# Combining the expert sums at the end of a mixture-of-experts layer on VectorE and GpSimd

## The reference, cut to what matters

```python
def trunk_layer(x, cond, lw, rope_a, rope_b, ctx):
    ...
    sh1, sc1, g1, sh2, sc2, g2 = jnp.split(mod, N_MOD, axis=-1)
    ...
    x = x + g1 * a
    h = rmsnorm(x, lw['norm2_g']) * (1 + sc2) + sh2
    b, s, d = h.shape
    x = x + g2 * moe_ffn(h.reshape(b * s, d), lw).reshape(b, s, d)
    return x, ctx_out

def moe_ffn(h, lw):
    ...
    routed = routed_experts(h, idx, w, lw['w_e1'], lw['w_e3'], lw['w_e2'])
    return routed + swiglu(h, lw['w_s1'], lw['w_s3'], lw['w_s2'])
```

## Time and profile before

| | |
|---|---|
| median of 3 runs | 1682.61 us (1682.14 to 1683.42) |
| the profiled execution, its own time | 1688.23 us |
| its span, first to last instruction | 1686.5 us |
| TensorE busy | 1541.8 us (91%) |
| VectorE busy | 1015.5 us (60%) |
| ScalarE busy | 723.2 us (43%) |
| GpSimd busy | 669.1 us (40%) |
| granted TensorE clock, mean | 0.973 |

### The profile page before, as it was taken

How to read it: one execution, slowest core, us unless ns; L and a number is a source line. 1 busy time by engine, 2 the same in 40 slices (tenths; PEclk the granted TensorE clock), 3 DMA queues, 4 the chain that set the end, 5 groups by cost and what they waited for, 6 DMA issues and landing times.

```text
span 1686.5 us, 25448 instructions
## 1 busy us (share of the span) xinstructions
PE 1541.8 (91%) x7703; PEld 1170.6 (69%) x7704; DVE 1015.5 (60%) x1601; ACT 723.2 (43%) x1067; POOL 669.1 (40%) x728
## 2 busy tenths in 40 slices
PE   8799798889989999999988999999999999999991
PEld 2678687778879999984544676666666666666660
DVE  1966688666666546544753666666656655665554
ACT  2523344334333222211212666666666655655550
POOL 0444277232214223310253355544546545544440
PEclk9899899989999999999999999999999999999996
DMA  9311100000006546527146888999999999999975
GB/s 326 106 61 43 38 1 1 1 1 1 1 26 176 150 133 217 150 80 255 38 188 218 294 280 295 323 352 341 338 336 356 335 328 339 353 331 327 336 241 199
DMA packets 126834, 333.71 MB, mean 198 GB/s; under 512 B 21140, under 2 KB 76568, under 8 KB 102040
## 3 DMA queue, kind: packets, MB, share of 16 engines
q1 hardware_dynamic: 104536, 288.09, 46.4%
q0 software_dynamic: 21440, 42.04, 10.2%
q10 hardware_dynamic: 784, 2.65, 0.4%
HBM read 316.54 MB, written 47.95 MB: 216 GB/s over the span
## 4 chain that ended last, share of the span: by engine, by line
DMA 30%; PE 18%; DVE 2%; issue 2%; SPq 1%; another core or an unknown queue 1%; ACT 1%; ACTq 0%; DVEq 0%; POOL 0%; POOLq 0%
DMA mem<-in_w_e 29%; PE psum L1746 4%; PE psum L2227 4%; PE psum L1608 2%; PE psum L2208 2%; PE psum L2210 2%; PE psum L2209 2%; SPq L2134 1%; PE psum L2216 1%; PE psum L1966 1%; DMA sums<-mem,si 1%; PE psum L1767 0%; DVE e_wlo L2322 0%; DMA mem<-sums 0%
## 5 line engine op out<-in xcount | busy, mean ns | idle before, releaser
L2322 DVE TENSOR_TENSOR e_wlo<-mem,e_whi 128x2048 fp32r<-128x2048 f32 x140 | 314.6, 2289 | 174.9 <-ACT e_whi L1922 174.8
L1922 ACT ACTIVATE e_whi<-mem 128x2048 fp32r (+1 forms) x140 | 260.5, 1908 | 104.7 <-SPq L2127 79.3
L2227 PE MATMUL psum<-mem 128*128 x560 | 253.4, 595 | 10.8 <-ACT mem L2290 10.8
L2164 POOL TENSOR_TENSOR held<-nhalf 1x1 f32<-1x1 f32 x206 | 144.5, 702 | 295.0 <-ACT mem_h L2282 144.2
L2208 PE MATMUL psum<-e_whi,e_xhi 128*128 128x512 f32 x560 | 228.1, 407 | 2.9 <-DVE e_xlo L2330 2.9
L2210 PE MATMUL psum<-e_wlo,e_xhi 128*128 128x512 f32 x560 | 222.2, 397 | 0.0
L2209 PE MATMUL psum<-e_whi,e_xlo 128*128 128x512 f32 x560 | 222.0, 397 | 0.0
L2227 PEld LDWEIGHTS psum<-mem 128*128 128x128 f32 x560 | 100.9, 190 | 114.7 <-issue 114.5
L1494 POOL TENSOR_TENSOR w_lo<-mem,w_hi 128x1024 fp32r<-128x1024 f32 x30 | 77.5, 2603 | 159.1 <-ACT w_hi L1438 159.1
L2208 PEld LDWEIGHTS psum<-e_whi,e_xhi 128*128 128x128 f32 x560 | 105.7, 189 | 25.7 <-issue 2.4
L2210 PEld LDWEIGHTS psum<-e_wlo,e_xhi 128*128 128x128 f32 x560 | 105.5, 188 | 25.6
(11 more groups left out here) (326 smaller groups left out, 3296.6 us busy)
## 6 DMA issues: line engine op xcount, KB each, us to landing
mem<-in_w_e SPq DMA_DIRECT2D x192, 1024.0 KB
mem<-in_w_mod SPq DMA_DIRECT2D x24, 1024.0 KB, 12.1
mem<-in_w_in SPq DMA_DIRECT2D x16, 512.0 KB, 4.6
mem<-in_w_in SPq DMA_DIRECT2D x3, 2048.0 KB, 8.7
sums<-mem SPq DMA_DIRECT2D x10, 512.0 KB
mem<-sums SPq DMA_DIRECT2D x10, 512.0 KB, 8.1
mem<-in_x_sample SPq DMA_DIRECT2D x8, 512.0 KB, 11.1
mem<-in_w_oa SPq DMA_DIRECT2D x8, 512.0 KB, 5.9
```

The costliest lines, as they stand in the source:

```text
L1922: act.activation(wHi13[b][:, a].rearrange("p k n -> p (k n)"), raw, ACT.Copy).then_inc(se["h13"], 1)
L2164: pool.tensor_tensor(held[:, c:c + 1], nhalf[0:1, 0:1], nhalf[0:1, 0:1], ALU.add)
L2227: mm = pe.matmul(pY[:, c * 512:(c + 1) * 512], gT[:, f, :], rows_.rearrange("p o w -> p (o w)"), start=(f == 0), stop=(f == 1))
L2322: dve.tensor_tensor(wLo13[b][:, a].rearrange("p k n -> p (k n)"), raw, wHi13[b][:, a].rearrange("p k n -> p (k n)").bitcast(F32), ALU.subt ...
```

## The change

All five tiles of the first sum are now multiplied by the gate and added to the residual as they land, on VectorE. The second sum is multiplied by the gate and added in a second pass: its tiles 2, 3 and 4 by VectorE, its tiles 0 and 1 by GpSimd, behind its last scatter. GpSimd counts on a new semaphore `s_cp`. The stores are issued in the order 2, 0, 3, 1, 4, each waiting on the engine that finishes that tile. Tiles 2 to 4 take four operations instead of three: the gate is applied to each sum rather than to their sum.

```diff
--- before.py
+++ after.py
@@ -1914,7 +1914,9 @@
     s_yt = [[sem(f"s_yt{b}{t}") for t in range(NT)] for b in range(2)]
     s_cb = sem("s_cb")
     s_cc = sem("s_cc")
+    s_cp = sem("s_cp")
     s_fin = sem("s_fin")
+    TAIL_POOL, TAIL_DVE = (0, 1), (2, 3, 4)
 
     def round_w13(act, slot, b, a):
 
@@ -2198,6 +2200,12 @@
                 due(pool, guard(3), scatter)
 
             run(pool, step)
+            for n, t in enumerate(TAIL_POOL):
+                pool.wait_ge(s_yt[1][t], 16)
+                pool.tensor_tensor(yt[1][t], yt[1][t], g2b[:, min(t, 1), :], ALU.mult).then_inc(s_cp, 1)
+                pool.wait_ge(s_cp, 2 * n + 1)
+                pool.wait_ge(s_cb, 2 * t + 2)
+                pool.tensor_tensor(yt[0][t], yt[0][t], yt[1][t], ALU.add).then_inc(s_cp, 1)
 
         @block.tensor
         def _(pe):
@@ -2304,8 +2312,11 @@
 
 
             run(act, step)
-            for t in range(NT):
-                act.wait_ge(s_cc, t + 1)
+            for t in (2, 0, 3, 1, 4):
+                if t in TAIL_DVE:
+                    act.wait_ge(s_cc, TAIL_DVE.index(t) + 1)
+                else:
+                    act.wait_ge(s_cp, 2 * TAIL_POOL.index(t) + 2)
                 dst = O["yp"][0] if t == 0 else O["ys"][0, (t - 1) * P:t * P, :]
                 act.dma_start(dst, yt[0][t]).then_inc(s_fin, 16)
             act.wait_ge(s_fin, 16 * NT)
@@ -2347,24 +2358,16 @@
 
             lo_w13(0, 0, 0)
             run(dve, step)
-            for t in range(2):
+            for t in range(NT):
                 dve.wait_ge(s_yt[0][t], 16)
                 dve.tensor_tensor(yt[0][t], yt[0][t], g2b[:, min(t, 1), :], ALU.mult).then_inc(s_cb, 1)
                 dve.wait_ge(s_cb, 2 * t + 1)
                 dve.tensor_tensor(yt[0][t], yt[0][t], x1[:, t, :], ALU.add).then_inc(s_cb, 1)
-            for t in range(2):
+            for n, t in enumerate(TAIL_DVE):
                 dve.wait_ge(s_yt[1][t], 16)
                 dve.tensor_tensor(yt[1][t], yt[1][t], g2b[:, min(t, 1), :], ALU.mult).then_inc(s_cb, 1)
-                dve.wait_ge(s_cb, 5 + t)
+                dve.wait_ge(s_cb, 2 * NT + n + 1)
                 dve.tensor_tensor(yt[0][t], yt[0][t], yt[1][t], ALU.add).then_inc(s_cc, 1)
-            for t in range(2, NT):
-                dve.wait_ge(s_yt[0][t], 16)
-                dve.wait_ge(s_yt[1][t], 16)
-                dve.tensor_tensor(yt[0][t], yt[0][t], yt[1][t], ALU.add).then_inc(s_cb, 1)
-                dve.wait_ge(s_cb, 2 * t + 3)
-                dve.tensor_tensor(yt[0][t], yt[0][t], g2b[:, 1, :], ALU.mult).then_inc(s_cb, 1)
-                dve.wait_ge(s_cb, 2 * t + 4)
-                dve.tensor_tensor(yt[0][t], yt[0][t], x1[:, t, :], ALU.add).then_inc(s_cc, 1)
 
 
 def rope_tables(width):
```

## The result

The changed kernel takes 1686.14 us (median of 7 runs) where the kernel before takes 1682.14 us (median of 7 runs beside it): the ratio is 1.003, its 95% interval 1.0018 to 1.0043. The prediction was 1687.2 us, slower. The profiled execution took 1686.29 us, its span is 1684.5 us.

The account below looks back on a forecast made before the run. VectorE's thirteen operations after the second sum's first landing were taken to set the end. Terms -4.29 + 8.64 + 0.2 = +4.55 us on 1682.61 gave 1687.2 us; range 1683.5 to 1690.0, the theory's own 1686.3 to 1688.4.

Parts of the forecast that it names:

- The new order on VectorE: In the tail, first-sum pairs fill VectorE's wait for the second sum, so its line ends earlier: -4.29 us.
- GpSimd in VectorE's line: In the tail, each of GpSimd's four two-input operations holds VectorE up by 2.16 us: +8.64 us.
- The turns: In the tail, GpSimd's and VectorE's operations alternate, four VectorE ones taking about 3.4 us, its last six 1.22.
- The stores: At the tail's end, tiles 3 and 1 go out together ahead of tile 4, delaying the last store: +0.2 us.
- rival C: In the tail, VectorE runs unbroken and GpSimd starts only behind it: +6.7 us, 1689.3 us; chance 0.08.
- B: In the tail, engines take turns but GpSimd's operations cost like cheaper f32 products: +2.5 us, 1685.1 us; chance 0.15.
- The stretch before the last scatter: Before 1652 us: a move of over a microsecond would mean the time is made elsewhere, a sign against the forecast.
- A: In the tail, both engines run side by side and nothing is held up: -4.3 us, 1678.3 us; chance 0.11.
- The turning point of 1.07 us: In the tail, the change wins if each GpSimd operation costs VectorE less than 1.07 us.

Follow-up runs that it names:

- e2_no_gpsimd: The changed kernel without GpSimd's four operations (output tiles 0 and 1 lack the second sum); ratio 0.9976 to the kernel before.
- e4_psum: The changed kernel with the gate copied to PSUM by ScalarE behind the loop and VectorE's products in PSUM; ratio 0.9995 to the kernel before.
- e6_psum_early: As e4_psum, but the gate is copied to PSUM inside the loop, so VectorE need not wait; ratio 0.998 to the kernel before.
- e1_all_vector: The changed kernel with the second sum's tiles 0 and 1 back on VectorE, stores in tile order; ratio 1.0006 to the kernel before.
- e10_one_input: The changed kernel with GpSimd's four operations replaced by one-input multiplications with a constant; VectorE ends 28.63 us after the last scatter's start, ratio not measured.
- e8_gate_only: The changed kernel with the gate read from PSUM but VectorE's products back in SBUF; VectorE ends 29.85 us after the last scatter's start, ratio not measured.
- e3_pool_kinds: The changed kernel with GpSimd's operations replaced by two memsets and two one-input multiplications; VectorE ends 28.88 us after the last scatter's start, ratio not measured.
- e7_psum_share: As e6_psum_early, with GpSimd also taking the first sum's tile 1; median 1676.46 us, ratio 0.9974 to the kernel before.
- e9_one_input_free: As e6_psum_early, with GpSimd's four operations replaced by one-input multiplications; VectorE ends 25.94 us after the last scatter's start, ratio not measured.

## Why the prediction was right

- **The new order on VectorE** (forecast -4.29 us). Measured apart by e2_no_gpsimd: -4.67, of which 0.34 is a first sum's tile 1 that landed earlier (8.91 us from the scatter against 9.25). The pairs run at 2.40 us start to start as in the earlier trace rows.
- **GpSimd in VectorE's line** (forecast 4 x 2.16 = +8.64). Measured 3.24 + 3.35 + 3.24 + 3.36 - 4 x 1.22 = 8.31 in the trace after, 8.40 against e2_no_gpsimd. I took 2.16 from a subtraction of 2.41 us; these are 2.35 long by e4_psum and e6_psum_early, and the hold-up is 2.08. The choice of L1494 over the cheaper products of the earlier trace rows was the one that mattered: with 1.90 us the sum would have been +2.5.
- **The turns.** They alternate strictly, as at 50 us. One detail was off: five VectorE operations at 1.22 are left behind GpSimd's last, not six; the fourth long one is already on the second sum (1671.60). The sum doesn't change by it.
- **The stores** (forecast +0.2). From VectorE's end to the span's end it is 3.49 us after and 3.10 before, +0.39. It goes with the order of the stores, not with GpSimd: 3.46 in e2_no_gpsimd, which has the new order without GpSimd's work, and 3.04 in e1_all_vector, which has the old one.
- **The sum**: +4.55 forecast, +4.12 in the traces from the scatter on (-4.67 + 8.40 + 0.39), +4.0 in the medians. No term is off by more than 0.4 us. The median lands this near in part by luck: its interval of 3.0 to 7.2 us would also fit rival C's +6.7, and B's +2.5 lies just outside. What rules these out are the tails. The median, 1686.14 us, lies 0.16 us below the range given to the theory itself (1686.3 to 1688.4), though a shift of 4.0 us lies in it: the kernel before came out at 1682.14 with more runs, 0.47 us below the 1682.61 that the forecast started from.
- **What would have told otherwise.** The stretch before the last scatter did move, by 6.12 us in the profiled executions, which I had named as a sign that the time is made elsewhere. That sign was badly chosen. Single executions of one kernel differ by as much (1683.37 to 1690.32 us for the changed one), and the profiled execution of before is a late one, 1688.23 us against a median of 1682.14. In the six kernels with a ratio in the table, the ratio agrees within 1 us with the difference of the span's ends from the scatter on.
- **The rivals.** A, side by side, would have put the end at 26: that is what e6_psum_early has, where none of VectorE's operations beside GpSimd has two SBUF inputs. B fell with GpSimd's 2.35 us. C fell with the turns: GpSimd waited less than one VectorE operation each time. The turning point of 1.07 us for each GpSimd operation is bracketed, by single traces: e10_one_input, at 0.72 each, ends 1.8 us before the kernel before; e8_gate_only, at 1.0 each (2.58 + 3 x 2.12 - 4 x 1.22 = 4.06 in all), 0.6 before it; the change, at 2.1 each, behind it.

## What to carry to other kernels

Before work goes to an idle GpSimd, look what VectorE does beside it: where VectorE's operations have two inputs in SBUF and GpSimd's read SBUF, each two-input operation of GpSimd's stands in VectorE's line with most of its length (2.1 of 2.35 us), and that is more than the move takes off (1.22 us). Where each of VectorE's operations has at most one input in SBUF (here with gate and products in PSUM), its operations are as short as before (1.22 us), nothing is held up, and the move pays: the same twenty operations end at 26.02 us on two engines (e6_psum_early) and at 30.94 on VectorE alone (e1_all_vector). With the gate alone in PSUM the end is 29.85 us (e8_gate_only), since the additions are still held up. An instruction that is longer than the same one elsewhere, without a gap before it, can be a wait; the busy share calls it work.

## What the runs showed of the hardware

- A one-input operation on GpSimd (128x1024 f32, times a constant) is slower than a two-input one when undisturbed, 2.77 us against 2.35, and yet holds VectorE up far less, 0.72 us against 2.1. The Trainium skill, "SBUF — State Buffer", section "Who interferes with whom", has the pair held for the whole instruction; the two-input operations come near that, the one-input ones don't. It fits that GpSimd gives way as soon as it has read its inputs, but no run shows when it reads. The same section of the Trainium skill says that a GpSimd operation which only writes does not contend with VectorE's two SBUF inputs; the memsets of e3_pool_kinds agree.
- ScalarE's first operation behind the loop starts 8.09 us after its last one in the loop in e4_psum, and the same in e6_psum_early, e7_psum_share, e8_gate_only and e9_one_input_free. The query for waits calls this "issue". It is branching, which doesn't count as busy: the loop's code goes on to 104 blocks where this run has 70. In e4_psum, between ScalarE's two operations (instruction, count, ns min/median/max, first and last start us):

```profile
L2120 ACTq COMPARE_BRANCH  x18: 45/45/45, 1647.6 to 1650.5; - x18
L2109 ACTq COMPARE_BRANCH  x9: 48/53/53, 1650.7 to 1655.4; - x9
```

L2120 is the test in front of each part of a block (`with eng.If(cond)`), L2109 the head of the loop over four blocks at a time. Between its first and its ninth pass here lie eight rounds for blocks that don't exist, about 0.6 us each (1650.7 to 1655.4). The copy at 1655.55 starts behind the last pass. Whoever puts work for ScalarE behind such a loop should count on it.
